# Query-key products of a cache attention over 256 columns, a rounded mask in the prompt attention, and query units of 320 columns

## The reference

```python
z = rmsnorm(x) @ w_in                       # q | k | v | indexer | conv input | gates
q, k = rmsnorm(q), rmsnorm(k)               # per head, 8 heads x 128
# prompt: an indexer scores all keys, the best 64 of each query stay
logits = q @ k.T * 128 ** -0.5 + bias       # keys that were not chosen: -1e30
o = softmax(logits) @ v
# sampled rows: the same against 1024 cached keys and 8 new ones, best 256
h = x + (sigmoid(ga) * (o @ w_a) + sigmoid(gb) * conv) @ w_out
h = h + swiglu(rmsnorm(h))
y_prompt = h_prompt[16:]                    # the meta tokens are dropped
```

## Time and profile before

| | |
|---|---|
| median of 3 runs | 2070.9 us (2069.2 to 2075.6) |
| profiled execution | 2070.0 us, of which the span of its instructions 2068.5 |
| PE, DVE, ACT, POOL busy | 97%, 60%, 43%, 8% of the span |
| mean granted clock of PE | 0.989 |

### The profile page before, as it was taken

How to read it: one execution, slowest core, us unless ns; L and a number is a source line. 1 busy time by engine, 2 the same in 40 slices (tenths; PEclk the granted TensorE clock), 3 DMA queues, 4 the chain that set the end, 5 groups by cost and what they waited for, 6 DMA issues and landing times.

```text
span 2068.5 us, 40223 instructions
## 1 busy us (share of the span) xinstructions
PE 2013.7 (97%) x14485; PEld 1926.7 (93%) x14485; DVE 1238.0 (60%) x2288; ACT 879.4 (43%) x1645; POOL 167.6 (8%) x296
## 2 busy tenths in 40 slices
PE   6998999999999999999999999999999999999997
PEld 5968999899987779999999999999999999999997
DVE  5338896566668998855655555544455554455553
ACT  5335444443344333355445544533344433344443
POOL 6300000111112210010000000000000000000012
PEclk9998999999999999999999999999999999999999
DMA  9374543677778984556555555555555555555573
GB/s 241 96 131 132 137 143 102 189 227 238 236 225 295 324 282 131 155 143 196 158 145 145 158 145 146 156 145 147 157 143 153 152 143 155 149 144 158 144 206 109
DMA packets 545590, 350.68 MB, mean 170 GB/s; under 512 B 15203, under 2 KB 524411, under 8 KB 545104
## 3 DMA queue, kind: packets, MB, share of 16 engines
q1 hardware_dynamic: 518480, 263.55, 47.3%
q0 software_dynamic: 25920, 84.68, 12.8%
q10 hardware_dynamic: 1088, 1.05, 0.2%
HBM read 338.91 MB, written 10.83 MB: 169 GB/s over the span
## 4 chain that ended last, share of the span: by engine, by line
PE 69%; DVE 0%; ACT 0%; DMA 0%; issue 0%; POOL 0%; POOLq 0%; DVEq 0%; ACTq 0%
PE psG L1423 21%; PE psG L1424 21%; PE psG L1425 21%; PE psS L1420 2%; PE psM L1423 1%; PE psM L1424 1%; PE psM L1425 1%; PE psT L1417 0%; PE psM L1417 0%; DMA vst<-in_cache_v 0%; DVE OL L1292 0%; PE psM L1420 0%; PE psM L1785 0%; ACT WH L569 0%; ACT utok L786 0%
## 5 line engine op out<-in xcount | busy, mean ns | idle before, releaser
L957 DVE TENSOR_TENSOR WL<-RAW,WH 128x512 fp32r<-128x512 f32 (+1 forms) x996 | 674.8, 692 | 630.8 <-ACT WH L569 629.1
L569 ACT ACTIVATE WH<-RAW 128x512 fp32r<-128x512 f32 (+1 forms) x996 | 614.1, 628 | 831.7 <-PE psG L1425 773.8
L1423 PE MATMUL psG<-XH,WH 128*128 128x320 f32 (+1 forms) x2688 | 852.6, 317 | 3.1 <-DVE WL L957 2.1
L1424 PE MATMUL psG<-XL,WH 128*128 128x320 f32 (+1 forms) x2688 | 838.7, 312 | 0.0
L1425 PE MATMUL psG<-XH,WL 128*128 128x320 f32 (+1 forms) x2688 | 837.2, 311 | 0.0
L1423 PEld LDWEIGHTS psG<-XH,WH 128*128 128x128 f32 x2688 | 507.4, 189 | 36.1 <-issue 26.6
L1424 PEld LDWEIGHTS psG<-XL,WH 128*128 128x128 f32 x2688 | 507.4, 189 | 1.6 <-issue 0.2
L1425 PEld LDWEIGHTS psG<-XH,WL 128*128 128x128 f32 x2688 | 507.5, 189 | 0.0
L1423 PE MATMUL psG<-MH,WH 128*128 128x320 f32 x960 | 298.1, 310 | 0.3 <-DVE ML L1392 0.3
L1425 PE MATMUL psG<-MH,WL 128*128 128x320 f32 x960 | 296.8, 309 | 0.0
L1424 PE MATMUL psG<-ML,WH 128*128 128x320 f32 x960 | 296.8, 309 | 0.0
(11 more groups left out here) (348 smaller groups left out, 1639.9 us busy)
## 6 DMA issues: line engine op xcount, KB each, us to landing
RAW<-in_w_in SPq DMA_DIRECT2D x160, 512.0 KB, 5.2
RAW<-in_w_ffn_down SPq DMA_DIRECT2D x96, 512.0 KB, 5.0
RAW<-in_w_ffn_gate SPq DMA_DIRECT2D x88, 512.0 KB, 4.6
RAW<-in_w_ffn_up SPq DMA_DIRECT2D x88, 512.0 KB, 4.8
kst<-in_cache_k POOLq DMA_DIRECT2D x64, 512.0 KB, 4.6
vst<-in_cache_v POOLq DMA_DIRECT2D x64, 512.0 KB, 6.0
RAW<-in_w_out SPq DMA_DIRECT2D x32, 512.0 KB, 4.8
RAW<-in_w_attn_br SPq DMA_DIRECT2D x16, 512.0 KB, 4.8
```

Of the source, the lines that this page charges most:

```text
L569: act.activation(WH[:, s % 2, 4 * r:4 * r + 4, c], RAW[:, s, 4 * r:4 * r + 4, c], ACT.Copy).then_inc(hi_done, 1)
L957: dve.tensor_tensor(WL[:, s, k, c], RAW[:, s, k, c], WH[:, s % 2, k, c].bitcast(F32), ALU.subtract).then_inc(lo_done, 1)
L1423: pe.matmul(out, WH[:, s % 2, k], hi, start=start, stop=False)
L1424: pe.matmul(out, WH[:, s % 2, k], lo, start=False, stop=False)
```

## The change

Three things are changed, and the places of many tiles with them.

In the cache attention kTs holds four pages, two to each chain, and PE makes the 16 products once for every four pages (after the last step of each s) over 256 columns, where it made them after every second page over 128. In the prompt attention the mask is written rounded (fp32r) to maskR, which lies where Wp lies, and the identity beside it is a rounded copy, identR, that ACT makes at the start; the mask product becomes one of rounded fp32. The eight query units multiply columns 16 to 335 only, into the same columns of the accumulator. For that PE's group 1 is taken out of the loop into straight code, and the loop runs over groups 2 and 3.

```diff
+    ("identR", [P, P], F32R, ST_A, ST_PROMPT),
-    ("kTs", [P, 2, H, P], F32, ST_KOUT, ST_CZ),
+    ("kTs", [P, 2, H, 2, P], F32, ST_KOUT, ST_CZ),
...
-PLACING = ("oT bNw iwtok Ss cmp Ws sqa SGA ...
+PLACING = ("bT7 SGA prow xtok osb iqx Ws vT ...
...
+    T["maskR"] = nc.alloc_sbuf_tensor_at("maskR", [P, 2, NP], F32R, offset=where["Wp"])
...
             act.activation(stat[:, 4:7], stat[:, 0:3], ACT.Sqrt, ...)
+            act.activation(identR[:], ident[:], ACT.Copy)
...
-  act.activation(kTs[:, j % 2, 0:4, :], TB[0]...)
+  act.activation(kTs[:, j % 2, 0:4, j // 2, :], TB[0]...)
...
-                dve.tensor_scalar(Wp[:, qt, 0:nk], Wp[:, qt, 0:nk], NEG / SC, None, ALU.mult)
+                dve.tensor_scalar(maskR[:, qt, 0:nk], Wp[:, qt, 0:nk], NEG / SC, None, ALU.mult)
...
-  dve.tensor_copy(kTs[:, j % 2, 4:8, :], TB[1]...)
+  dve.tensor_copy(kTs[:, j % 2, 4:8, j // 2, :], TB[1]...)
...
-            def x_quarter(G_, s, r, first_col=0):
+            def x_quarter(G_, s, r, first_col=0, at=0):
-                         lambda k: split_mm(G[s % 2][:, 0:NT - first_col], s, k, XH[:, k, first_col:NT], ...
+                         lambda k: split_mm(G[s % 2][:, at:at + NT - first_col], s, k, XH[:, k, first_col:NT], ...
...
+            def q_quarter(s, r):
+                x_quarter(G0["qk"] + s // 4, s % 4, r, T0C, T0C)
...        # the query quarters in the indexer's stage: x_quarter(G0["qk"], s, r) -> q_quarter(s, r)
-                lagged(G0["qk"] + g, lambda G_, s: x_all(G_, s) if s >= multiplied else None, squares)
+                def main(G_, s):
+                    if isinstance(g, int):
+                        for r in range(4) if s >= multiplied else ():
+                            q_quarter(4 * g + s, r)
+                    else:
+                        x_all(G_, s)
+                lagged(G0["qk"] + g, main, squares)
             qk(0, 2)
-            with pe.Fori(1, GN["qk"]) as g:
+            qk(1)
+            with pe.Fori(2, GN["qk"]) as g:
                 qk(g)
...
-                mm(out, ident[:], Wp[:, qt, 0:keys_of(qt)], False, True).then_inc(p_qk, 1)
+                mm(out, identR[:], maskR[:, qt, 0:keys_of(qt)], False, True).then_inc(p_qk, 1)
...
                         pe.wait_ge(kc_A, n + 2)
                         pe.wait_ge(kc_D, n + 2)
-                        if n % 2 == 0:
-                            continue
-                        if g and t % 4 == 0:
-                            pe.wait_ge(lg_done, 2 * g - 1 + t // 4)
-                        for k in range(4):
-                            for r in range(4):
-                                h = 4 * (r % 2) + k
-                                ins = mm(SB[t // 4][32 * r:32 * r + 32, P * (t % 4):P * (t % 4) + P], qsz[:, h, 2 * g + r // 2, :], kTs[:, r // 2, h, :], k == 0, k == 3)
-                        if t % 4 == 3:
-                            ins.then_inc(kq_done, 1)
+                    if g and s % 2 == 0:
+                        pe.wait_ge(lg_done, 2 * g - 1 + s // 2)
+                    for k in range(4):
+                        for r in range(4):
+                            h = 4 * (r % 2) + k
+                            ins = mm(SB[s // 2][32 * r:32 * r + 32, 2 * P * (s % 2):2 * P * (s % 2) + 2 * P], qsz[:, h, 2 * g + r // 2, :],
+                                     kTs[:, r // 2, h].rearrange("p t n -> p (t n)"), k == 0, k == 3)
+                    if s % 2:
+                        ins.then_inc(kq_done, 1)
```

More of the change, by code:

```diff
@@ L199 @@
     ("rl", [P, 2, PAST], F32, ST_INDEX, ST_INDEX), ("rln", [P, NS], F32, ST_INDEX, ST_INDEX), ("rp", [P, 4, NP], F32, ST_INDEX, ST_INDEX),
[L201 removed]
+    ("QK", [P, 2 * H, NT], F32, ST_QK, ST_KOUT), ("identR", [P, P], F32R, ST_A, ST_PROMPT),
     ("sq", [P, 2, NT], F32, ST_QK, ST_QK), ("rt", [P, 2, NT], F32, ST_QK, ST_QK),
@@ L207 @@
     ("ktok", [P, 2, 3, 2 * P], F32, ST_V, ST_KOUT), ("qsz", [P, H, B, 32], F32, ST_V, ST_CZ),
-    ("kst", [P, 4, CC], F32, ST_V, ST_CZ), ("kTs", [P, 2, H, P], F32, ST_KOUT, ST_CZ),
+    ("kst", [P, 4, CC], F32, ST_V, ST_CZ), ("kTs", [P, 2, H, 2, P], F32, ST_KOUT, ST_CZ),
     ("sgt", [P, NT], F32, ST_PROMPT, ST_CZ), ("cblk", [NS, NS], F32, ST_CZ, ST_SOFTMAX),
@@ L221 @@
 ]
-PLACING = ("oT bNw iwtok Ss cmp Ws sqa SGA osb vs QK csq e8 gsb PTn utok uss Wp qm rln bT7 ub rf pairM IW cms ikTa rt hT "
-           "ut ML esel xs L ikst Tb OH vtok xTs crt iqx SGB m8p qsz ktok v2 oh relb relx m8s vst kst ya vT kTs iktok Lp CH "
-           "wrow sel iqT yp iwT cblk xtok ikT gt ytok ustok sct sq2 iqs sgt rp sq at rl Sp prow pT CL ").split()
+PLACING = ("bT7 SGA prow xtok osb iqx Ws vT Tb Sp esel xTs cmp sqa identR cms Lp ytok ikTa crt vst kst gsb oh sgt kTs "
+           "ikst rl sq2 iwT wrow bNw ya m8p relx PTn at qm CH qsz iqT rf rt CL rln sct sq Ss rp Wp ustok pT iwtok xs m8s "
+           "vs ut cblk ktok csq yp L ub relb uss vtok iqs IW utok v2 gt OH iktok pairM ikT SGB e8 ML QK sel hT oT ").split()
 def layer(nc, I, O):
@@ L264, in layer @@
     ident, ones, zer, prm, gqk, wdw, eps, stat = (T[x] for x in ("ident", "ones", "zer", "prm", "gqk", "wdw", "eps", "stat"))
+    identR, maskR = T["identR"], T["maskR"]
     ptab, ptab2, biasR = T["ptab"], T["ptab2"], T["biasR"]
@@ L766, in cz @@
                         act.wait_ge(k_tr, g * 16 + (4 * s + j + 5))
-                        act.activation(kTs[:, j % 2, 0:4, :], TB[0][:].rearrange("p (h n) -> p h n", h=4), ACT.Copy).then_inc(kc_A, 1)
+                        act.activation(kTs[:, j % 2, 0:4, j // 2, :], TB[0][:].rearrange("p (h n) -> p h n", h=4), ACT.Copy).then_inc(kc_A, 1)
                         ahead_quarter(G0["cz"] + g, s, j)
@@ L1550, in _ @@
             keys(PAIRS - 1)
+            def q_quarter(s, r):
+                x_quarter(G0["qk"] + s // 4, s % 4, r, T0C, T0C)
             for r in range(2):
-                x_quarter(G0["qk"], 0, r)
+                q_quarter(0, r)
             pe.wait_ge(d_cpA, PAIRS)
@@ L1598, in _ @@
                 scores(p)
-                x_quarter(G0["qk"], *between[p])
+                q_quarter(*between[p])
                 total(p)
@@ L1605, in _ @@
             ins.then_inc(n_mm, 1)
-            x_quarter(G0["qk"], 1, 2)
+            q_quarter(1, 2)
             pe.wait_ge(d_rln, 1)
@@ L1622, in _ @@
                 if i == 15:
-                    x_quarter(G0["qk"], 1, 3)
+                    q_quarter(1, 3)
             pe.wait_ge(d_ss, 1)
@@ L1736, in cz @@
                     for j in range(4):
-                        n, t = g * 16 + (4 * s + j), (4 * s + j) // 2
+                        n = g * 16 + (4 * s + j)
                         pe.wait_ge(k_ld[j], g * 64 + 16 * (s + 1))
```

8 lines of the change are left out of this document (3 added, 5 removed).

## The result

The changed kernel takes 2056.9 us (median of 4 runs, 2056.6 to 2057.7), the kernel before 2071.7 beside it; the ratio is 0.9931, 95% interval 0.9918 to 0.9944. A second measurement, beside other kernels, gave 0.9930 (0.9916 to 0.9943). The profiled execution of the changed kernel took 2056.6 us, 13.4 less than that of the kernel before (2070.0); the medians lie 14.8 apart, and the forecast was 9.7 less.

A forecast was written before the change was run, and what follows sets the result against it. PE, busy for 97% of the span, was taken as the bound. Cache attention 4.6, masks 2.4 and query units 2.7 sum to 9.7 us off the profiled 2070.0, giving 2060.3 us; the 8-in-10 range was 2055.9 to 2065.4.

The forecast's parts named there:

- Cache attention: 64 cached pages: one cluster replaces two, saving a fixed 0.27 to 0.31 us 16 times; 4.6 us, bounds 0 and 5.0.
- Mask of 272 keys: Prompt attention: one rounded product replaces two full fp32 passes, saving 0.35 us each; eight made, first lost, 2.4 us.
- Mask of 144 keys: Prompt attention: rounded product of 144 columns taken to gain nothing over two full passes; 0, other end 1.3 us.
- The mask's write: DVE's first mask instruction, ahead of the first logits: still held until POOL's memset ends; 0, other end -1.4 us.
- Query units: Eight query units: 360 products 7.6 ns shorter each, first 24 counting nothing; 2.7 us, or 0.5 if DVE can't follow.
- The rest: PE's loop, ACT's identity copy and new SBUF places: counted as nothing, up to 0.5 us either way for the loop.
- A price that goes with the columns: Rival, cache attention: the cluster's 0.27 to 0.31 us grow with columns, so nothing is won there; 2064.9 us, 10%.
- Narrow products cheap or the write free: Rival, prompt attention masks: 144 keys gain 1.3 us, the write runs free for 1.4, or both; 2057.6 to 2059.0 us, 17%.
- DVE as the bound: Rival, query units: DVE becomes the bound there; 2062.5 us, 7%.
- The clock in the cache attention: Rival, slower: PE's clock falls to 1.2 GHz in clusters, 1.7 us each; 10 falls 2077.3 us, all 16 2087.5; 4%.

The follow-up runs named there:

- e2: Changed kernel with cache attention and query units put back as in the kernel before, leaving the rounded masks alone; ratio to the kernel before 0.9976.
- e3: Changed kernel with cache attention and masks put back as in the kernel before, leaving the query units' change alone; ratio to the kernel before 0.9974.
- e10: Kernel before with only the change's places in SBUF and its two unused names; ratio to the kernel before 0.9999.
- e4: Changed kernel with the masks of 144 keys back in full fp32, those of 272 still rounded; 2058.1 us, ratio to the kernel before 0.9933.
- e5: Changed kernel plus a sweep of rounded and full fp32 products of 64 to 272 columns ahead of the first logits; rounded ones took about 0.112 us at least.
- e6: Changed kernel with POOL waiting for both of DVE's masks before it clears qsz; 2057.1 us, ratio to the kernel before 0.9930.
- e11: Changed kernel unaltered, run again with a second profile; 2056.2 us.
- e8: Changed kernel with one cluster of 512-column passes for eight pages instead of four; stage 1.8 us shorter than in the changed kernel, cluster 3.72 us.
- e12: Changed kernel with POOL waiting for the masks, run again with a second profile; 2056.9 us, ratio to the kernel before 0.9929.

## Why the prediction was right, and where it wasn't

The forecast was 2060.3 us, range 2055.9 to 2065.4; 2056.9 lies in it, near its lower end, and the kernel is faster by over 0.3%. From the profiled time the sum was 9.7 us against 13.4. That the time still lies inside the range is in part luck: its lower end was made of cheap narrow products (1.3), a mask's write that runs free (1.4) and one fall of the clock fewer (1.7). The write did not run free; 1.0 at the end of a stage came instead, from a term that the sum didn't have.

- **Cache attention**, 4.6: 32 x 1.16 - 16 x 2.02 = 4.8 in the pages. The split of the earlier trace rows into columns and a fixed 0.27 to 0.31 was right, with 0.30. Not in the sum was the end of the stage: DVE's last multiplications (ub, 0.43 and 0.21 us) now lie beside a cluster that is 0.9 longer, and PE's wait at the end falls from 1.8 to 1.25. The sum had no term for that wait. The prediction said that a cut of PE's work is worth nothing where PE waits; it is worth something where what PE waits for also moves under PE's work. With the 0.4 by which the stage of before was longer than e2's, e3's and e10's, and which may be the places', that makes 5.8, above the bound of 5.0 that the prediction gave.
- **Mask of 272 keys**, 7 x 0.35 = 2.4: the column to the burst shrinks by 3.23 between e3 and after, 0.94 of it for the 144 keys (e4), so 2.3 for these. That the first is lost was right: PE turns the softmax at 299.62, just when DVE has scaled it (299.27 + 0.29), and has waited for ACT's copy of vT until 299.07.
- **Mask of 144 keys**, taken as 0 between 0 and 1.3: this step failed; it is 0.94. I read the four products of the earlier trace rows as 1.84 ns a column, and the rival named what may be right: a price per product with new weights. The step is about 0.112 us at any width up to 240 columns (e5). Rows of another width would have told: the 8-column passes of relx in the kernel before, 0.132 each with weights of 128 columns, are not cheaper than the products of 64.
- **The mask's write**, 0 between 0 and -1.4: right. It is held as before, as by the two pages of the Trainium skill that the prediction names there ("SBUF — State Buffer", "SBUF: two separate sides", and "VectorE: DVE Perf Modes", "What auto-detection actually checks"), and e6 shows that POOL's memset holds it.
- **Query units**, 2.7: 2.4 to 2.6 (after, e11 and e3 against before). DVE isn't the bound; its last idle time before the mask is still 1.16 us, at 275.69, by a row like that of the earlier trace rows. The wait for the transfer took the first 24 products' gain, as said: 2.66 us now, 2.63 in the earlier trace rows.
- **The rest**, 0: the burst of short passes gave 1.25, the start of the kernel 0.3. The first was in no row that I read, though the range left room for a fall of the clock more or fewer. A stretch at half clock right behind the prompt attention was there to be seen in the kernel before, and a place where time can be had without a change of work belongs among the rivals.
- **Rivals.** A price that goes with the columns: ruled out by the cluster of 256 columns (2.02, not 2.32) and by e8. Narrow products cheap or the write free: half of it came, the narrow products. DVE as the bound: no. The clock in the cache attention: 1.00 from 386 to 592 us, with clusters twice as long.

The sum of the differences: 0.3 start, 0.2 cluster, 1.0 rest of that stage, 1.1 masks (0.9 by those of 144 keys, the rest by the lower clock at 297 us that is gone), 1.25 burst, less 0.3 in the query units, 0.1 behind: 3.7, which is 13.4 - 9.7.

## What to carry to other kernels

Before a price per column is read from a narrow product, look for a second width with the same weights: a step that doesn't change with the width is a price per product, and then making products wider is free, up to the width at which their columns take longer, and making them narrower useless. What is fixed in a tiled cluster is paid per tiled stretch, so gather the columns in one stretch, and look what other engines can then do beside the longer stretch. A microsecond won ahead of a stretch of short products can be lost again in the clock of that stretch, as in the profiled executions of e6 and e12, so a gain is counted at the end of the next dense stage and not where it arises.

## What the runs showed of the hardware

- A floor of 0.112 us for a product with weights of 128 fp32 columns at granted clock 1.00, for rounded and full fp32 passes alike, and of 0.213 at 0.50 for rounded ones (e5). The burst's passes, with weights of 32 columns in four chains side by side, lie under it: 128 in 1.92 us.
- The clock can fall while PE is busy without a gap: in e5 it fell to 0.50 at 303 us, 3 us into products of 64 and 96 columns with PE busy in 8.90 of 8.90 us ahead, stayed there for 13.7 us through 96 to 224 columns, and was back at 1.00 in the 224s. A narrow product cost nearly twice its floor there.
- 0.30 us per tiled stretch of 32-column weights, whether it has 32 or 64 passes and 128, 256 or 512 columns.
- A DVE write of rounded fp32 beside a POOL memset took 1.70 us, alone 0.23.
